# Half of the samples' value pages issued by GpSimd's queue, and the samples' probabilities turned two steps later

## The reference

```python
s = q . cmp_k            # 32 compressed blocks: softmax, o_cmp, and the blocks' importance
idx = top_k(score, 16)   # selected blocks of 64 keys
o_sel = softmax(q . ksel) @ vsel      # for a sample: of its 8 pages of cache_sel_v
o_win = softmax(q . kw) @ vw          # the last 512 keys
o = g0 * o_cmp + g1 * o_sel + g2 * o_win
y = x + (o * silu(gate)) @ w_out
```

## Time and profile before

| what | value |
|---|---|
| median of 3 runs | 969.73 us (968.93 to 972.0) |
| time of the profiled execution | 969.1 us |
| its span, first to last instruction | 967.4 us |
| PE busy | 910.7 us, 94% of the span |
| DVE / ACT / POOL busy | 474.6 / 293.1 / 232.3 us |
| mean granted clock of PE | 0.982 of full speed |
| chain that ended last | PE 82%, DVE 5%, SP's queue 5%, ACT 3%, DMA 2% |

### The profile page before, as it was taken

The page is one execution under the profiler, slowest core; times in us unless marked ns, Lnnn a source line. Parts: engine busy times, 40 slices in busy tenths (PEclk is TensorE's granted clock), DMA queues, the critical chain, the costliest instruction groups (busy, mean ns, idle before and its releaser), DMA issues.

```text
span 967.4 us, 15863 instructions
## 1 busy us (share of the span) xinstructions
PE 910.7 (94%) x5210; PEld 483.4 (50%) x5210; DVE 474.6 (49%) x965; ACT 293.1 (30%) x716; POOL 232.3 (24%) x321
## 2 busy tenths in 40 slices
PE   6999999999899998999999999998999997976998
PEld 3544444444455553545565666466554454443444
DVE  1157778779445543212234261715677777653211
ACT  5101111013354541032101111424555666543100
POOL 0000223210034330340424242001344443333000
PEclk9999999999999999999999999999999999898999
DMA  9243665593145467772414132030212241132211
GB/s 352 66 164 101 228 235 172 200 287 85 44 146 159 136 205 254 253 191 90 144 35 145 39 134 86 13 89 12 63 48 60 72 111 64 46 92 61 90 45 45
DMA packets 86070, 117.61 MB, mean 122 GB/s; under 512 B 21006, under 2 KB 49886, under 8 KB 85678
## 3 DMA queue, kind: packets, MB, share of 16 engines
q1 hardware_dynamic: 66432, 80.97, 25.5%
q0 software_dynamic: 9920, 27.31, 9.6%
q10 hardware_dynamic: 9648, 8.41, 2.7%
HBM read 108.70 MB, written 11.36 MB: 124 GB/s over the span
## 4 chain that ended last, share of the span: by engine, by line
PE 82%; DVE 5%; SPq 5%; ACT 3%; issue 2%; DMA 2%; ACTq 0%; DVEq 0%
PE ps L720 26%; PE ps L977 11%; PE ps L983 6%; PE ps L1280 6%; PE ps L729 3%; PE ps L1000 3%; PE ps L1039 3%; PE ps L915 3%; PE ps L1151 2%; PE ps L1162 2%; PE ps L893 2%; SPq L329 2%; SPq L330 2%; PE ps L865 2%; DMA arena<-cache_sb_v 2%
## 5 line engine op out<-in xcount | busy, mean ns | idle before, releaser
L720 PE MATMUL ps<-wring,arena 128*128 128x512 f32 x448 | 197.5, 600 | 1.5 <-issue 1.5
L720 PEld LDWEIGHTS ps<-wring,arena 128*128 128x128 f32 x448 | 84.9, 192 | 105.5 <-issue 105.5
L668 POOL TENSOR_TENSOR z<-z,work 128x1024 f32<-128x1024 f32 (+1 forms) x64 | 80.2, 1252 | 191.6 <-DVE work L1994 191.4
L977 PE MATMUL ps<-wring,z 128*128 128x512 f32 (+2 forms) x320 | 106.7, 488 | 0.0
L1512 ACT ACTIVATE z<-ps,work 128x512 f32<-128x512 f32 (+3 forms) x128 | 66.3, 523 | 69.9 <-DVE work L1986 67.3
L1335 ACT ACTIVATE z<-ps 128x512 f32<-128x512 f32 (+1 forms) x64 | 27.4, 433 | 181.8 <-PE ps L720 147.6
L977 PEld LDWEIGHTS ps<-wring,z 128*128 128x128 f32 x320 | 54.8, 190 | 43.4 <-issue 41.8
L359 POOL DMA_DIRECT2D arena<-cache_sb_k x64 | 34.4, 537 | 164.9 <-DVE work L1629 141.1
L1834 DVE TENSOR_TENSOR arena<-ps,consts 128x512 f32<-128x512 f32 x32 | 30.3, 1020 | 82.3 <-PE ps L1017 82.3
L1523 ACT ACTIVATE arena<-ps 128x512 f32<-128x512 f32 (+3 forms) x128 | 49.1, 438 | 31.6 <-PE ps L1151 31.6
L1791 DVE TENSOR_TENSOR xres<-xres,ps 128x512 f32<-128x512 f32 (+1 forms) x32 | 15.5, 483 | 86.5 <-PE ps L1280 38.9
(11 more groups left out here) (319 smaller groups left out, 1245.0 us busy)
## 6 DMA issues: line engine op xcount, KB each, us to landing
wring<-w_in SPq DMA_DIRECT2D x12, 2048.0 KB, 9.7
arena<-cache_sb_k POOLq DMA_DIRECT2D x64, 256.0 KB, 3.0
arena<-cache_sb_v SPq DMA_DIRECT2D x64, 256.0 KB, 3.6
wring<-w_out SPq DMA_DIRECT2D x3, 2048.0 KB, 8.0
arena<-cache_sel_k SPq DMA_DIRECT2D x64, 64.0 KB, 1.8
consts<-cache_sel_v SPq DMA_DIRECT2D x64, 64.0 KB, 1.8
consts<-aux SPq DMA_DIRECT2D x1, 2315.5 KB, 16.0
xres<-x_prompt SPq DMA_DIRECT2D x4, 512.0 KB, 9.3
```

What stands on the lines that cost most here:

```text
L668: nc.gpsimd.tensor_tensor(P_u(n), P_u(n), bc(coef(n).unsqueeze(2), [P, 2, (NT - n % NT) * P]), ALU.mult).then_inc(n_scaled, 1)
L720: mm = pe.matmul(ps[:, t, 0:width], stat, mov, start=(k == 0), stop=(k == KT - 1))
L977: mm = pe.matmul(ps[:, bank, at:at + w], normed1(k, t), wring[:, slot, k, lo:lo + w], start=(k == 0), stop=(k == KT - 1))
```

## The change

It has two parts. First, the eight pages of each sample's values are split: SP issues the first four, POOL the last four, with semaphores of their own (two that POOL's earlier page loads used, counted on from `sv_pool_base`). POOL issues samples 0 and 1 in its steps 32 and 33, right behind `scale(33)` and `scale(34)`, and sample b from 2 on in step 46 + 2b, right behind `scale(47 + 2b)`. Second, the turns of the samples' probabilities move from steps 43 to 45 to steps 45 to 47, the eight products with values from steps 47, 49, ... 61 to steps 49, 51, ... 63, and on ACT the exponential of `P_win` and the small one move from step 41 to step 43.

```diff
@@ -288,6 +288,7 @@
                    [z[:, NT, P_OFF + j * 512:P_OFF + (j + 1) * 512] for j in range(2)]
         NRING = len(cm_pages)
         cm_loaded = [sem(f"cm_loaded{j}") for j in range(NRING)]
+        sv_pool_loaded, sv_pool_base = cm_loaded[0:2], 64 * (-(-4 * NB // NRING))
         cm_turned, cm_T, cmp_turned, cmp_T, cm_proj, cm_sq, cm_mean, cm_rstd, ckT_ready, cvT_ready, cvT_paired = (
             sem("cm_" + x) for x in ("turned", "T", "p_turned", "p_T", "proj", "sq", "mean", "rstd", "ckT", "cvT", "cvT_paired"))
         cv_turned, cv_ready, kz_turned, kz_T, kz_swapped, kz_ready, ck_copied = (
@@ -432,8 +433,8 @@
                 return z[:, i // 2, GATE + (i % 2) * SEQ:GATE + (i % 2 + 1) * SEQ]
 
             KEY_STEPS = {1: [(0, 0), (0, 1)], 2: [(0, 2)], 3: [(0, 3)], 5: [(1, 0), (1, 1)], 6: [(1, 2)], 7: [(1, 3)]}
-            VALUE_STEPS = {47: 0, 49: 1, 51: 2, 53: 3, 55: 4, 57: 5, 59: 6, 61: 7}
-            PTURN_STEPS = {43: 0, 44: 1, 45: 2}
+            VALUE_STEPS = {49 + 2 * b: b for b in range(NB)}
+            PTURN_STEPS = {45: 0, 46: 1, 47: 2}
 
             SB_STEPS = [(i, s) for i in range(NHP) for s in reversed(range(NT))]
             NSTEP = len(SB_STEPS)
@@ -547,8 +548,7 @@
                 def load_values(b):
 
                     sp.wait_ge(sv_used, b - 1) if b > 1 else None
-                    for q in range(2):
-                        page_group(sp, "cache_sel_v", b * NPG + 4 * q, vsets[b % 2][q], sv_loaded[b % 2])
+                    page_group(sp, "cache_sel_v", b * NPG, vsets[b % 2][0], sv_loaded[b % 2])
 
                 sp.wait_ge(bank_free, 5 + 80)
                 sp.dma_start(d_g, z[0:NB, NT, BG:BG + 3 * HN]).then_inc(r_sent, 16)
@@ -677,10 +677,19 @@
                     nc.gpsimd.tensor_tensor(pc, pc, bc(cst("cmp_one").rearrange("p (t n) -> p t n", t=NT).unsqueeze(2), [P, NT, 2, NPB]),
                                             ALU.mult).then_inc(nc_p, 1)
 
+                def load_values(b):
+
+                    pool.wait_ge(sv_used, b - 1) if b > 1 else pool.wait_ge(cm_proj, 4)
+                    page_group(pool, "cache_sel_v", b * NPG + 4, vsets[b % 2][1], sv_pool_loaded[b % 2])
+
                 scale(0)
                 for n in range(NUNIT):
                     if n + 1 < NUNIT:
                         scale(n + 1)
+                    if n in (32, 33):
+                        load_values(n - 32)
+                    if n - 1 in VALUE_STEPS and VALUE_STEPS[n - 1] + 2 < NB:
+                        load_values(VALUE_STEPS[n - 1] + 2)
                     if n % 8 == 2:
                         cmp_scale(n // 8)
 
@@ -1220,7 +1229,8 @@
                     rows_b = slice(32 * (b // 2), 32 * (b // 2) + 32)
                     pe.wait_ge(sk_PT, 3)
                     take(7, sv_T, b + 1)
-                    pe.wait_ge(sv_loaded[b % 2], 144 * (b // 2 + 1))
+                    pe.wait_ge(sv_loaded[b % 2], 80 * (b // 2 + 1))
+                    pe.wait_ge(sv_pool_loaded[b % 2], sv_pool_base + 64 * (b // 2 + 1))
                     for q in range(3):
                         for m in range(4):
                             n = 4 * q + m
@@ -1555,6 +1565,7 @@
                     if n == 41:
                         act.wait_ge(*marks_dve.at("sk_max"))
                         st.done(nc.scalar.activation(P_sel, P_sel, ACT.Exp, bias=stats[:, 8:9], accum_out=stats[:, 12:13]))
+                    if n == 43:
                         st.done(nc.scalar.activation(P_win, P_win, ACT.Exp, bias=stats[:, 9:10], accum_out=stats[:, 13:14]))
                         nc.scalar.activation(stats[:, 14:16], stats[:, 6:8], ACT.Exp).then_inc(*marks_act.next("sk_exp"))
                     if n in VALUE_STEPS and VALUE_STEPS[n] + 2 < NB:
```

## The result

The changed kernel takes **964.02 us** (median of 5 runs, 962.66 to 966.08) against 969.73 before: a ratio of 0.9941 (95% interval 0.9931 to 0.9952), 5.7 us less, where 11.8 had been forecast. It is faster and inside the range of 951 to 968, but by only half of the sum.

A forecast was written before the change was run, and what follows sets the result against it. PE bounds the kernel, waiting in the last third for value pages that SP issues too slowly. Terms of -17.4, +1.7, +4.4, +0.5, +4.2 and -5.2 sum to -11.8 us, so 957.9 us for the median, range 951 to 968.

The forecast's parts named there:

- SP's issuing was the pace: Samples 2 to 7: SP needs 8.8 us a sample to issue pages, PE's own work 6.5; halving the issuing gives -17.4 us.
- The step from ACT's queue to POOL's: POOL assumed to issue as ACT's queue does: pages start where a `scale` starts, four taking 4.56 us.
- All three costs of the pages to `turn_cmp`: Waits of `turn_cmp` for POOL at steps 36, 52 and 60: some 3, 2 and 3 us.
- The stretch: Rival: POOL's issues stretch while DVE is busy; at 2.0 us a page 975.5 us; chance 0.1.
- the 1.3 that the prediction had called wrong: Sign against the forecast: pages on POOL more than 1.3 us apart.
- The turns' term: Steps 40 to 48: later turns give -5.2 us, of which idle -1.6 and slow work -3.6; between 0 and -8.3.
- The signs that it named for being right: Among them: page waits within 1 us, `turn_cmp` waiting 3, 2 and 3 us, first turn's wait under 2 us.
- a long wait adds about 1.3 us of work at the lower clock: PE behind long waits: 24 matmuls take 1.51 us for 0.86, the values product 1.55 for 0.87.
- the three long waits of before: Values products waiting for pages 3.50, 4.37 and 3.8 us; slow work behind them put at 3 x 1.3 = 4.0 us.
- The part on POOL's half: POOL's pages delay what is queued behind them: +1.7 and +4.4 us at `cmp_scale`, +0.5 for landing, +4.2 for samples 0 and 1.
- the part on the turns: Steps 41 to 45: the first turn's wait behind ACT's copy and exponentials shrinks; 3.1 us of shorter waits remain there; -5.2 us.

The follow-up runs named there:

- e6: e5 with the exponential of `P_win` and the small one back at ACT's step 41; 950.56 us.
- e3: The changed kernel with SP issuing all pages of samples 0 and 1, POOL only the second halves of samples 2 to 7; 958.5 us.
- e2: The split of the pages alone: the changed kernel with turns, products and exponentials at their old steps; 966.58 us.
- e4: e3 with `cmp_scale` ahead of POOL's four pages where both lie in one step; 960.24 us.
- e1: The later turns, products and exponentials alone: the kernel before with the second part of the change, SP issuing all pages; 964.63 us.
- e5: e3 with POOL's pages a step earlier, behind `scale(46 + 2b)` instead of `scale(47 + 2b)`; 950.39 us.
- e7: e5 with turns, products and exponentials at their old steps; 954.09 us.
- e8: e5 with the exponential of `P_win` and the small one at ACT's step 42 instead of 43; 950.83 us.

## Why the prediction was half right

**Right: what bounded, and how POOL issues.** SP's issuing was the pace, and halving it removed the page waits (13.4 to 0.4). The step from ACT's queue to POOL's held: pages from the start of a `scale`, 4.58 us for four against 4.56. All three costs of the pages to `turn_cmp` are within 0.3 us of the forecast. The stretch did not come: 1.14 to 1.16 us a page while DVE was busy for 36.14 of 60.58 us. One pair of pages, at 876.14 and 877.59, is 1.45 apart, more than the 1.3 that the prediction had called wrong; it is the only one. The turns' term was right in both its parts: slow work -3.6 as forecast, and the waits 0.7 better, with the first turn at 1.55. What e6 adds is that the moved exponentials, which the prediction counted with, had no part in it. The signs that it named for being right came almost all, and yet half of the sum was missing: none of them weighed slow work behind the new waits, or DVE.

**Wrong by size: "a long wait adds about 1.3 us of work at the lower clock".** The wait at step 36 cost 2.68 us and then 3.0 of slow work, at a granted clock of 0.58 for 8.2 us, in place of 1.3. This 1.7 is the larger part of the 5.56 that e3 took back, against 4.2. The 1.3 came from the 24 matmuls and the values product of the earlier trace rows, the first two rows of a slow stretch, not its whole. Busy PE of the whole stage, against the same work at full clock, gives 5.2 us for the three long waits of before, 1.7 each. That would have been nearer, but not the 3.0 here or the 2.8 behind the wait of 3.20: why these cost more stays open. In the third stage the two errors cancel, since the removed waits were worth more as well (-2.3 measured, -2.7 summed).

**Wrong by omission: what else is late behind POOL and behind the later turns.** The part on POOL's half followed only `cmp_scale` and `turn_cmp`, and the part on the turns ended at step 45 and at ACT. From step 48 on there are 2.6 us of idle PE that no term had: 1.11 at sample 0's product, 1.20 at 868.93, 0.28 at L1180. The second is the split's, through a `scale` that the pages displaced until it ran where DVE's L2005 was due: it is there in e2, e3 and e4, and not in e1 or e5. The first is the later turns', since it is there in e1 and not in e2 or e7, and so is the third, 0.28, in e1: their statistics (L2063) moved to where POOL's `scale(48)` runs, and take 1.47 us in e1, e5, e6 and the changed kernel, 0.62 in the kernel before and in e2, ahead of `cmp_max` and the product. The longer L2063 explains 0.85 of the 1.11 (1.47 less 0.62); that the rest comes of these statistics standing there at all is read from the order on DVE, and no run took them away by themselves.

These two make 1.7 and 2.6, less 0.6 of terms that came out better: the 3.7 between 11.8 and 8.1. The rest, 8.1 in the stages against 5.7 in the medians, is not the change's, as far as the traces tell: 1.7 is the later start of that part in this execution, and 0.7 the difference of a profiled execution to the median.

## What to carry to other kernels

When half of a queue's issues go to an engine that also computes, its total matters less than where the issues stand in its order: with the same later turns, kernels that split the pages of samples 2 to 7 were 5.7, 11 or 19 us faster than before by where POOL's issues stood, and the good place was the gap in which that engine waited for its next input. For each displaced instruction follow not just its reader but the engine that shares its memory ports, and the bank behind that. Price a wait's slow clock from the busy time of a whole stage against the same stage at full clock, not from the first instruction behind it.

## What the runs showed of the hardware

- **The clock's price is not fixed by the wait.** Behind 3.06 us of idle PE the second stage has 3.6 us of slow work in the kernel before and in e7, but 2.2 less in e2. Behind 1.1 us at sample 0's product the 24 matmuls took 1.51 in e1 and e5, and 0.86 in e3 and e6. The wait of 2.67 at the end of e2 left the next four at 0.66 and the slow work began about 2 us later; one of 3.20 in the changed kernel made them 1.12 at once. Executions of one kernel differ as well: e3's five took 954.0 us at a mean granted clock of 0.991 to 961.2 at 0.984, while e5, without the long waits, stayed within 1.1 us at 0.990 to 0.992. What decides stays open, and one profile's slow work is not the kernel's.
- **A page issue on POOL takes 1.14 to 1.15 us as a rule, of which only the last 0.54 stands in the engine's own row.** Where the rest could run beside tensor operations, four pages took 2.16 us (856.88, behind two scales).
- **Scatter ahead of the change.** The first of the three stages began at 782.30 us in the profile of before, and between 782.57 and 786.62 in the others, behind the same instructions; e3, e4, e5, e6 and e8, whose programs are the same up to there, lie between 782.79 and 786.62. A few us between single profiles of this kernel must be read by stage.
